# State-space stage of a two-layer decoder trunk: order of chunks, skip term, clears and products

## The reference, cut to what matters

```python
lam_bar = jnp.exp(lam * dt)
b_bar = ((lam_bar - 1.0) / lam)[..., None] * b
bu = jnp.einsum('gpn,bsgn->bsgp', b_bar, uf)
_, states = lax.associative_scan(combine, (a, bu), axis=1)   # x_t = lam_bar * x_(t-1) + bu_t
y = jnp.einsum('gnp,bsgp->bsgn', c, states).real + d_skip * uf
g = jax.nn.gelu(y)
out = g * jax.nn.sigmoid(g @ w_glu + b_glu)
```

## Time and profile before

| what | value |
|---|---|
| median of 3 runs | 1474.73 us (1473.92 to 1476.48) |
| the profiled execution | 1474.49 us, its span 1472.8 us |
| TensorE busy | 1439.1 us (98%) |
| VectorE busy | 1191.7 us (81%) |
| ScalarE busy | 978.0 us (66%) |
| GpSimd busy | 100.2 us (7%) |
| mean granted TensorE clock | 0.991 |
| DMA | 425.95 MB, mean 289 GB/s |

### The profile page before, as it was taken

One profiled execution on the slowest core, in us unless ns is written; L12 is line 12 of the kernel. 1 busy time (PEld: TensorE's weight loads), 2 busy tenths in 40 slices (PEclk: granted clock), 3 DMA queues, 4 the chain that ended last, 5 costly groups with the idle time before them and its releaser, 6 DMA issues.

```text
span 1472.8 us, 20745 instructions
## 1 busy us (share of the span) xinstructions
PE 1439.1 (98%) x7832; PEld 1209.2 (82%) x7832; DVE 1191.7 (81%) x1190; ACT 978.0 (66%) x954; POOL 100.2 (7%) x130
## 2 busy tenths in 40 slices
PE   8989999999989999999999999999999999999997
PEld 4678799998869888888888888888888888888886
DVE  6895455555777988988898898888889889888887
ACT  5326444444674777877777777787787777778775
POOL 1753100000240000000000000000000000000000
PEclk9999999999999999999999999999999999999999
DMA  8437655443326999999999999999999999999992
GB/s 230 145 71 260 236 192 185 147 155 115 121 109 233 349 370 371 331 362 375 337 351 360 348 357 366 378 323 363 373 337 358 366 343 349 370 373 331 359 376 94
DMA packets 193088, 425.95 MB, mean 289 GB/s; under 512 B 14002, under 2 KB 23088, under 8 KB 192944
## 3 DMA queue, kind: packets, MB, share of 16 engines
q1 hardware_dynamic: 192480, 424.35, 80.3%
q10 hardware_dynamic: 560, 0.94, 0.3%
HBM read 421.67 MB, written 1.05 MB: 287 GB/s over the span
## 4 chain that ended last, share of the span: by engine, by line
PE 91%; ACT 2%; POOL 1%; DVE 1%; issue 1%; ACTq 1%; DMA 1%; SPq 1%; DVEq 0%
PE bank L425 78%; PE bank L447 3%; PE bank L908 2%; PE bank L490 2%; PE bank L920 1%; PE bank L700 1%; PE bank L529 1%; PE bank L453 1%; ACTq L1021 1%; SPq L1081 1%; POOL work L1171 1%; ACT w_hi L1531 1%; DMA ring<-work 1%; PE bank L626 1%; DVE ring L1697 0%
## 5 line engine op out<-in xcount | busy, mean ns | idle before, releaser
L2015 DVE TENSOR_TENSOR w_lo<-ring,w_hi 128x2048 fp32r<-128x2048 f32 x341 | 777.7, 2290 | 99.6 <-ACT w_hi L1531 98.2
L1531 ACT ACTIVATE w_hi<-ring 128x2048 fp32r<-128x2048 f32 x341 | 649.1, 1917 | 129.1 <-PE bank L425 126.1
L425 PE MATMUL bank<-w_hi,xg_hl 128*128 128x512 f32 x1792 | 557.1, 392 | 0.0
L425 PEld LDWEIGHTS bank<-w_hi,xg_hl 128*128 128x128 f32 x1792 | 332.8, 188 | 67.2
L425 PE MATMUL bank<-w_lo,xg_hl 128*128 128x512 f32 x896 | 349.4, 390 | 0.0
L425 PE MATMUL bank<-w_hi,at_hl 128*128 128x512 f32 x896 | 277.5, 391 | 0.0
L425 PEld LDWEIGHTS bank<-w_lo,xg_hl 128*128 128x128 f32 x896 | 168.2, 188 | 35.8
L425 PEld LDWEIGHTS bank<-w_hi,at_hl 128*128 128x128 f32 x896 | 167.1, 188 | 33.9
L425 PE MATMUL bank<-w_lo,at_hl 128*128 128x512 f32 x448 | 174.5, 389 | 0.0
L1888 DVE TENSOR_TENSOR fpart_hl<-ring,fpart_hl 128x1024 fp32r<-128x1024 f32 x66 | 80.6, 1224 | 75.1 <-ACT fpart_hl L1439 74.9
L425 PE MATMUL bank<-ht_hl,fpart_hl 128*128 128x256 f32 x1056 | 128.0, 283 | 0.0
(11 more groups left out here) (253 smaller groups left out, 1151.7 us busy)
## 6 DMA issues: line engine op xcount, KB each, us to landing
ring<-in_l_moe_w_gate SPq DMA_DIRECT2D x58, 2048.0 KB, 8.0
ring<-in_l_moe_w_up SPq DMA_DIRECT2D x57, 2048.0 KB, 7.9
ring<-in_l_moe_w_down SPq DMA_DIRECT2D x56, 2048.0 KB, 7.9
ring<-in_l_ffn_w_gate SPq DMA_DIRECT2D x5, 2048.0 KB, 9.0
ring<-in_l_ffn_w_up SPq DMA_DIRECT2D x5, 2048.0 KB, 7.9
ring<-in_l_ffn_w_down SPq DMA_DIRECT2D x5, 2048.0 KB, 7.5
ring<-in_l_w_in SPq DMA_DIRECT2D x4, 2048.0 KB, 9.3
ring<-in_l_w_out SPq DMA_DIRECT2D x4, 2048.0 KB, 8.7
```

The lines of the kernel that those rows point to most:

```text
L425: last = mm(p, lhsT=xs[a], rhs=ws[b], start=start and q == 0, stop=stop and q == 2, **kw)
L1531: ac(w_hi(n), at(e_slot(q) * SLOT + j * HALF, HALF), ACT.Copy).then_inc(S("hi"), 1)
L2015: tt(LO[e_slot(q)][:, j * HALF:(j + 1) * HALF], at(e_slot(q) * SLOT + j * HALF, HALF), w_hi(n).bitcast(fp), ALU.subtract).then_inc(S("lo"), 1)
```

## The change

Chunk order: inside Ug, V, VX and Xbd the 32 chunks are ordered "(r b)", the step in a block outermost, so that the same step of all 8 blocks is contiguous. The Ug copies put them in that order as they read PSUM, and the gelu reads them back from it. Shifting by one chunk now takes two copies per half instead of one.

Skip term: 24 small products of an identity with MD (32 rows, 16 columns each) are added to K in PSUM; GpSimd's add is gone. K's products wait for the sums of CA by pairs instead of for all.

Tiles: Tm lies where Wt was, and Kst, Ysb and Xbd lie where Bm was, so that Tm can be cleared before V is computed. Clears: GpSimd clears half of Tm; ScalarE clears the other half in front of its V copies, and Xbd in two halves, in front of its K copies and in front of its Toeplitz DMAs.

Order: the queries' squares go behind the keys' ones, after the scan; the power steps go in front of the wait for V; on TensorE the carried products go in front of the Toeplitz ones, which now finish the banks; on GpSimd the first keys' root goes in front of the queries' one.

```diff
-        Tm = at(18432, 2, STEPS * PAIRS * GDIM)
+        Tm = at(B0, 2, STEPS * PAIRS * GDIM)
...
-        Kst = at(B0, STEPS, PAIRS, GDIM, rows=32)
+        Kst = at(18432, STEPS, PAIRS, GDIM, rows=32)
...
-        Ysb = at(B0, STEPS, PAIRS * GDIM, rows=64)
-        Xbd = at(B0 + 3072, 2, PAIRS, 64)
+        Ysb = at(18432, STEPS, PAIRS * GDIM, rows=64)
+        Xbd = at(18432 + 3072, 2, PAIRS, 64)
...
@@ tensor: K
-            pe.wait_ge(S("s5_ca"), 12)
+            pe.wait_ge(S("skip"), 1)
...
             for jq in range(6):
                 c0 = jq % 4 * P
+                pe.wait_ge(S("s5_ca"), 2 * jq + 2)
                 for ri in range(2):
                     for a in range(4):
                         mm(kb[jq // 4][32 * a:32 * a + 32, c0:c0 + GDIM], lhsT=W0bd[:, ri, jq * 4 + a], rhs=cT[:, ri, jq * 4 + a],
-                           start=(jq % 4 == 0 and ri == 0), stop=(ri == 1), skip_group_check=True)
+                           start=(jq % 4 == 0 and ri == 0), stop=False, skip_group_check=True)
+                for a in range(4):
+                    mm(kb[jq // 4][32 * a:32 * a + 32, c0:c0 + GDIM], lhsT=ident[0:32, 0:32], rhs=MD[:, jq * 4 + a],
+                       start=False, stop=True, skip_group_check=True)
...
@@ tensor: Y
+            yb = [unit(pe, ("Y", n), n) for n in range(3)]
+            pe.wait_ge(S("xbd"), 12)
+            for n in range(3):
...
+                            mm(yb[n][64 * jh:64 * jh + 64, a * P:(a + 1) * P], lhsT=Xbd[:, ri, j], rhs=CA[:, ri, j],
+                               start=(a == 0 and ri == 0), stop=False, skip_group_check=True)
             pe.wait_ge(S("tm"), 16 * 16)
...
-            pe.wait_ge(S("xbd"), 4)
...
@@ toeplitz
-            eng.wait_ge(S("kst_d"), 1)
-            eng.wait_ge(S("tm_zero"), 1)
+            for n in range(2):
+                read_out(eng, ("K", n))
+            eng.wait_ge(S("tm_zero"), 2)
...
@@ gpsimd
-            got(pool, ("V", 2))
-            g.memset(Tm, 0.0).then_inc(S("tm_zero"), 1)
-            g.memset(Xbd, 0.0).then_inc(S("xbd_zero"), 1)
-            for n in range(2):
-                read_out(pool, ("K", n))
-            g.tensor_tensor(Kst[:, 0], Kst[:, 0], MD, ALU.add).then_inc(S("kst_d"), 1)
+            got(pool, ("Bm", 11))
+            g.memset(Tm[:, 1], 0.0).then_inc(S("tm_zero"), 1)
+            root("mk0", 1, hss[:, 0:8], hrs[:, 0:8], HD)
             root("q0", 1, hss[:, 16:24], hrs[:, 16:24], HD)
-            root("mk0", 1, hss[:, 0:8], hrs[:, 0:8], HD)
...
@@ scalar
+            def clear(x, n):
+                return ac(x.rearrange("p (a b) -> p a b", b=P), ident.unsqueeze(1).to_broadcast([P, n // P, P]), ACT.Copy, scale=0.0)
...
-                    free(ac(Ug[:, n * 4:n * 4 + 16], p[:, :].rearrange("p (a c) -> p a c", a=16), ACT.Copy), ("Ug", n // 4))
+                    free(ac(Ug[:, n * 4:n * 4 + 16].rearrange("p a (r b) -> p a r b", r=SL),
+                            p[:, :].rearrange("p (a b r) -> p a r b", a=16, r=SL), ACT.Copy), ("Ug", n // 4))
...
+            act.wait_ge(S("s5_w0"), 4)
+            clear(Tm[:, 0], STEPS * PAIRS * GDIM).then_inc(S("tm_zero"), 1)
             for n in range(3):
                 p = got(act, ("V", n))
...
+            clear_carried(0)
             for n in range(2):
                 p = got(act, ("K", n))
...
+            clear_carried(1)
             toeplitz(act, 1)
             act.wait_ge(S("scan"), 1)
-            act.wait_ge(S("xbd_zero"), 1)
+            act.wait_ge(S("xbd_zero"), 2)
             for g2 in range(2):
-                ac(Xbd[g2 * 64:(g2 + 1) * 64, 1, :, g2 * 32 + 1:g2 * 32 + 32], VX[g2 * 64:(g2 + 1) * 64, 1, :, 0:31],
-                   ACT.Copy).then_inc(S("xbd"), 1)
+                g_ = slice(g2 * 64, (g2 + 1) * 64)
+                ac(Xbd[g_, 1, :, g2 * 32 + SB:g2 * 32 + CHUNKS], VX[g_, 1, :, 0:CHUNKS - SB], ACT.Copy).then_inc(S("xbd"), 1)
+                ac(Xbd[g_, 1, :, g2 * 32 + 1:g2 * 32 + SB], VX[g_, 1, :, CHUNKS - SB:CHUNKS - 1], ACT.Copy).then_inc(S("xbd"), 2)
...
-                    last = ac(GT6[:, g2 * 3 + n].rearrange("p (c k) -> p c k", k=STEPS),
-                              p[:, :].rearrange("p (k g c) -> p g c k", k=STEPS, g=2)[:, g2], ACT.Gelu_apprx_tanh)
+                    last = ac(GT6[:, g2 * 3 + n].rearrange("p (b r k) -> p b r k", r=SL, k=STEPS),
+                              p[:, :].rearrange("p (k g r b) -> p g b r k", k=STEPS, g=2, r=SL)[:, g2], ACT.Gelu_apprx_tanh)
...
@@ vector: steps_and_squares (the four lines go behind head_norm of "mk0", after the scan)
-                for h in range(2):
-                    for m in range(TM):
-                        read_out(dve, ("win0", h, m))
-                head_norm([(heads_of(HS[:, m, MAIN:D]), 4) for m in range(TM)], 8, "q0", 16, sq0, None)
...
-            for n in range(3):
-                read_out(dve, ("V", n))
             read_out(dve, "q_pw")
             next_powers(0, 1, 0)
             next_powers(0, 2, 1)
-            XB = VX.rearrange("p i j (b r) -> p (i j) b r", r=SL)
+            for n in range(3):
+                read_out(dve, ("V", n))
+            XB = VX.rearrange("p i j (r b) -> p (i j) r b", r=SL)
...
             for r in range(1, SL):
-                carry(0, 0, SB, XB[:, :, :, r - 1], XB[:, :, :, r])
+                carry(0, 0, SB, XB[:, :, r - 1], XB[:, :, r])
```

More of the change, by code:

```diff
@@ L660, in _ @@
             proj_kv("memkv1", MT[1], "mkv1", (6, 7))
+            yb = [unit(pe, ("Y", n), n) for n in range(3)]
+            pe.wait_ge(S("xbd"), 12)
+            for n in range(3):
+                for a in range(4):
+                    for ri in range(2):
+                        for jh in range(2):
+                            j = 8 * n + 4 * jh + a
+                            mm(yb[n][64 * jh:64 * jh + 64, a * P:(a + 1) * P], lhsT=Xbd[:, ri, j], rhs=CA[:, ri, j],
+                               start=(a == 0 and ri == 0), stop=False, skip_group_check=True)
             pe.wait_ge(S("tm"), 16 * 16)
-            yb = [unit(pe, ("Y", n), n) for n in range(3)]
             for n in range(3):
@@ L669, in _ @@
                             r0 = 64 * jh + 32 * g2
-                            mm(yb[n][r0:r0 + 32, a * P:(a + 1) * P], lhsT=Ug[:, g2 * PAIRS + j], rhs=Tj[:, g2, j],
-                               start=(a == 0), stop=False, skip_group_check=True)
-            pe.wait_ge(S("xbd"), 4)
-            for n in range(3):
[L674 to L679, removed]
+                            last = mm(yb[n][r0:r0 + 32, a * P:(a + 1) * P], lhsT=Ug[:, g2 * PAIRS + j], rhs=Tj[:, g2, j],
+                                      start=False, stop=True, skip_group_check=True)
                 ready(last, ("Y", n))
@@ L1327, in _, with clear_carried @@
                 free(ac(dst, src, ACT.Copy), ("V", n))
+            def clear_carried(ri):
+                clear(Xbd[:, ri].rearrange("p j c -> p (j c)"), PAIRS * 64).then_inc(S("xbd_zero"), 1)
+            clear_carried(0)
             for n in range(2):
@@ L1730, in steps_and_squares @@
                     v.tensor_copy(U5[:, :, s * GDIM:(s + 1) * GDIM], U4[:, s].rearrange("p (g i) -> p g i", i=GDIM)).then_inc(S("u5_dve"), 1)
-                for q in range(4):
-                    read_out(dve, ("memT", q))
-                for h in range(2):
-                    for m in range(TM):
-                        read_out(dve, ("win0", h, m))
-                head_norm([(heads_of(HS[:, m, MAIN:D]), 4) for m in range(TM)], 8, "q0", 16, sq0, None)
             for ri in range(2):
@@ L1784, in _ @@
             for r in range(1, SL):
-                carry(0, 0, SB, XB[:, :, :, r - 1], XB[:, :, :, r])
+                carry(0, 0, SB, XB[:, :, r - 1], XB[:, :, r])
             for b in range(1, SB - 1):
-                carry(SL - 1, b, 1, XB[:, :, b - 1:b, SL - 1], XB[:, :, b:b + 1, SL - 1])
+                carry(SL - 1, b, 1, XB[:, :, SL - 1, b - 1:b], XB[:, :, SL - 1, b:b + 1])
             for r in range(SL - 1):
-                carry(r, 1, SB - 1, XB[:, :, 0:SB - 1, SL - 1], XB[:, :, 1:SB, r])
+                carry(r, 1, SB - 1, XB[:, :, SL - 1, 0:SB - 1], XB[:, :, r, 1:SB])
             v.memset(stp[:, 0, 0, 0:1], 0.0).then_inc(S("scan"), 1)
@@ L1792, in _ @@
             for g2 in range(2):
-                v.tensor_copy(Xbd[g2 * 64:(g2 + 1) * 64, 0, :, g2 * 32 + 1:g2 * 32 + 32],
-                              VX[g2 * 64:(g2 + 1) * 64, 0, :, 0:31]).then_inc(S("xbd"), 1)
+                g_ = slice(g2 * 64, (g2 + 1) * 64)
+                v.tensor_copy(Xbd[g_, 0, :, g2 * 32 + SB:g2 * 32 + CHUNKS], VX[g_, 0, :, 0:CHUNKS - SB]).then_inc(S("xbd"), 1)
+                v.tensor_copy(Xbd[g_, 0, :, g2 * 32 + 1:g2 * 32 + SB], VX[g_, 0, :, CHUNKS - SB:CHUNKS - 1]).then_inc(S("xbd"), 2)
             dve.wait_ge(S("ld_hg"), 192)
@@ L1803, in _ @@
             head_norm([(heads_of(MKR[0].rearrange("p a b -> p (a b)")), 8)], 8, "mk0", 0, sqk, None)
+            for h in range(2):
+                for m in range(TM):
```

(3 more changed lines are left out.)

## The result

The changed kernel takes 1464.2 us (median of 5, 1462.86 to 1468.32) beside 1474.79 us in the same comparison: ratio 0.9932, 95% interval [0.9915, 0.9948]. So the gain is 6 to 10 us, and 7 to 8 is the better estimate (medians of all 18 executions of the changed kernel 1466.5 us, of the 78 of the kernel before in the later comparisons 1474.2); 3.3 were forecast. The profiled execution took 1466.02 us, its span is 1464.3.

The account below looks back on a forecast made before the run. TensorE, last to end, bounds the kernel for 91% of the span. Its products start at 104.1 instead of 107.44 us, 3.3 us gained with nothing added behind: 1471.4 us from 1474.73, range 1468.8 to 1474.6.

Parts of the forecast that it names:

- the products' own time: TensorE's Toeplitz and carried products: the clock falls again in 2.8 us of idling, so they stay at 9.7 us.
- ScalarE, instruction by instruction: ScalarE's copies and clears priced singly; query copies (1.07) and a clear (1.5) precede its Toeplitz issues, which start at 91.85.
- SP's head start: SP's Toeplitz issues start 2.5 us ahead, shortening ScalarE's 11.29 us queue stay by up to 2.5; middle: free at 102.0.
- rival B: TensorE idles less before the Y products and the clock doesn't fall: 6.0 us gained, 1468.7 us; chance 0.10.
- The skip term: 24 small products joining K on TensorE cost 0.6 us, at most 1.7; GpSimd's add (1.00) and its wait fall away.
- The start of the stage: Moving the queries' squares on VectorE: K gains 0.25 of 1.9 us, V stays, scan starts 1.8 us earlier, about 83.1.
- The scan: VectorE's scan, contiguous instead of at a step of four floats: 24.2 us become 18.1, saving 6.1, ending at 101.2.
- Rival D: The step isn't what slows VectorE's scan, but the repeated coefficient or port: scan stays 24.2 us, 1476.7 us; chance 0.08.
- The clears and copies: ScalarE's clears cost 2.8 us (Tm half) and 1.5 (Xbd half), Ug copies nothing more, its four Xbd copies 2.04.
- Behind Y: After the Y products nothing is added or lost; ScalarE's 1.28 us table load stays in the chain.

Follow-up runs that it names:

- e6: Changed kernel with ScalarE waiting for its own two Xbd clears in front of its Toeplitz DMA issues instead of behind them: 1469.1 us, ratio 0.9970.
- e8: Changed kernel with the queries' squares back in front of the CA products: ratio 0.9961 to the kernel before.
- e7: Changed kernel with the skip term added by GpSimd again and without the 24 small products: ratio 0.9958 to the kernel before.
- e3: Changed kernel with the chunks in natural order again (scan at a step of four floats, one shifting copy): ratio 1.0014 to the kernel before.
- e10: Same kernel as e7 (changed kernel, skip term on GpSimd again), run once more: ratio 0.9964 to the kernel before.
- e13: Kernel before, with 22 unread identity products in TensorE's wait in front of the Toeplitz products: 1472.0 us beside 1473.5, ratio 0.9992.
- e11: Changed kernel with the skip term on GpSimd again and 26 unread identity products in TensorE's wait: ratio 0.9958 to the kernel before.
- e1: The kernel before, unchanged, run and traced once more: ratio 1.0001.
- e2: The changed kernel, unchanged, run and traced once more: ratio 0.9950 to the kernel before.
- e9: The changed kernel, unchanged, as the measure for other runs of its call: ratio 0.9940 to the kernel before.
- e5: Kernel before plus the chunk layout alone, with its copies and the gelu's reading: ratio 1.0000.

## Why the prediction was wrong

The direction and the mechanism held: both chains had to move, the scan's and the DMAs', and Y starts behind ScalarE's copies. Two steps failed. The larger in us is the products' own time: the forecast put the clock's share at nothing, and it measured 1.5 to 2.8 us. The other is ScalarE's issues, put behind copies that they don't wait for. Together with V's place in the first trace it made Y's start 1.5 us too late. These are the terms:

- **ScalarE, instruction by instruction: a failed step.** The forecast let ScalarE "first copy the queries (1.07) and clear (1.5)" before its DMA issues, at 91.85. Nothing makes them wait: an issue goes out when its own semaphores are met, beside copies that were started or queued ahead of it. The issue stood 0.08 us behind the last K copy. Put right with the forecast's own numbers, the queue is free at 89.2 + 0.1 + 11.3 = 100.6, the scan's 101.2 counts, and Y starts at 103.3: +38.5 instead of +39.3, so 0.8 us of the 1.5 by which +39.3 missed +37.8. The other 0.7 is the start of the scan, below. e6, with the wait written in, shows the price of a real one (2.4 us).
- **SP's head start.** It fell away with the same step: both queues start together, and ScalarE's is held for 11.3 us as before, ending with the scan to 0.1 us. Where the head start exists (e6) it is worth 0.5 us and not the 1.2 that is in the middle of 102.0.
- **The products' own time: the larger failed step.** The forecast kept 9.7 us, since it saw 2.8 us of idling in the new kernel. The wait was 0.3 us, and all four traces of the changed kernel took 8.2. Of the kernel before the traces have 9.7 and 11.0. So what came is rival B, which had a chance of 0.10: the clock stayed up, 1.5 to 2.8 us, after a shorter wait than even B assumed (2.0). That the shorter wait is the reason is supported and not shown: the clock fell in the waits of 2.9 (e8), 3.5 (e7) and 5.4 us (e3), and not in those of 0.3 to 2.2 us (e6 the longest), but not in e10's 3.8 either. Its start of 103.3 is also what the step above gives when put right. That the products' gain is passed on to the end is supported by e13's median and not shown by its interval.
- **The skip term.** Forecast 0.6 us, at most 1.7; measured 2.6 to 2.8 (e7, e10): each of the six groups is 0.30 us longer, and 0.7 to 1.1 us is a gap among the L582 products of the last group for which no trace names a releaser. It stands in all four traces of the changed kernel, and at this place in none of those without the small products (e7, e10, e11); its cause is open. The mis-sizing did no harm, since TensorE waited there anyway. It is also why TensorE's wait shrank to 0.3 us: without it (e7, e10) the wait is 3.5 to 3.8 us and the clock falls in one trace of two.
- **The start of the stage.** V was forecast not to move, and it stands at +10.5 in the traces of both kernels (e1, e2), and at +11.7 only in the first one, which had the stretch at half clock. By this the forecast, worked out from the first trace, had the scan's start at +18.3 (83.1) where it was at +17.6: the 0.7 us named above. The move of the squares, priced at 0.25 us for K and 1.8 for the scan, was worth 2.3 us at the start of the scan and the same at Y, and nothing for K (e8). K starts 1.6 to 2.2 us earlier (+16.3 for +17.9 to +18.5), with the squares back as without; what is left for that is its waiting for the sums by pairs, which no run undoes.
- **The scan.** Forecast 18.1 us, measured 18.1. Of the 6.1 us the layout gave 5.4 (e3 takes 23.5); the other 0.7 is one add that took 1.62 us instead of 0.90 beside GpSimd's skip-term add (at 90.4 us in the first trace). GpSimd's add is gone from the changed kernel; with it back (e7), the scan is 0.7 us longer again. Rival D fell with e3 and with the rows. The power steps took 0.8 us more than before, beside GpSimd's last sums, and the scan started 0.6 us behind the last V copy (80.35 to 80.94).
- **The clears and copies.** 2.76 and 1.48 us for 2.8 and 1.5; Ug's copies kept 0.60 us at the new step; the four Xbd copies took 1.86 for 2.04. The Toeplitz products didn't wait.
- **Behind Y** nothing was added up to the gated unit, and the table load is on the chain, as forecast; it is worth 0.3 to 0.7 us and not 1.28, as the next thing is TensorE's transposes. The profiled execution alone lost 1.6 us to half clock in the gated unit, the like of what e13's rival foretold; the three later traces of the changed kernel did not.

The trace agrees with one half of the note that the prediction weighed (the Trainium skill, SBUF — State Buffer, section "Door 1: The DMA port swizzle"): a step of four floats never hits a 16-byte line twice, and costs 1.9 ns an element instead of 1.04. It disagrees with the other half, that four fp32 elements may be stridden for free.

In sum, on the traces: 4.9 us of earlier start (+42.7 to +37.8) and 1.5 to 2.8 us of clock, 6.4 to 7.7 us, beside 6.4 to 7.4 us between the medians of the three later comparisons. The granted clocks of the single executions say the same in another way, and account for the surplus of the first comparison (10.6 us) as far as it can be seen. At a mean clock of 0.994 both kernels occur: 14 executions of the kernel before with a mean of 1472.0 us, 6 of the changed one with 1467.5, so 4.5 us at equal clock, near the 4.9 of Y's start. Over all, the kernel before has 0.987 to 0.994 and a mean of 1474.1 us, the changed one 0.993 to 0.997 and 1466.1. So some 3.5 of the 8.0 us go with a higher clock; this is an estimate, as the clocks have three places. They are not all won in the Y products: a stretch at half clock near 160 us stands in all four traces of the kernel before and its variants, and near 150 in only two (e2, e9) of the four of the changed one. In the first comparison three of five executions had 0.997 (1462.9 to 1464.2 us), in the later ones three of 13 (1464.3 to 1464.6). Why one execution gets 0.997 and another 0.994 stays open.

## What to carry to other kernels

Where two chains end within a few microseconds of each other, price the change against both: here each half alone was worth nothing, in the order of products that it had, and the pair about 0.5%. A DMA issue of ScalarE waited here for its semaphores and for the issues ahead of it, and not for the copies that precede it in the engine's program (0.08 us behind the last K copy, and 2.5 with a semaphore in between); look at whether a semaphore stands between before pricing them in. And an engine's wait has two prices, its length and the clock that the engine has afterwards.

## What the runs showed of the hardware

- VectorE, fp32 in SBUF: with the 0.16 us that the forecast worked out as fixed taken off, a step of 16 bytes costs 1.8 to 1.9 ns an element on a product (1576 ns for 768 in e3, 1636 in the trace of before) and on an add (891 ns for 384 in e3), contiguous ones 1.04 (958 ns for 768). ScalarE reading PSUM at the same step pays nothing (0.60 us for 512 elements, as before).
- A VectorE product or add of two SBUF tiles beside GpSimd's add of 1.0 us took 0.7 to 0.8 us longer: 1.62 us for 0.90 (before), 1.15 for 0.34 (e5), 1.24 for 0.56 (e7). Beside GpSimd's clear of Tm the scan's instructions kept their times (0.56 and 0.90 us in the trace of before).
- 24 products of 32 rows and 16 columns, packed between other small ones, cost 2.6 to 2.8 us of TensorE (e7, e10); the cheapest row for such a product would have made it 0.5. Of this 1.8 is in the groups (0.81 us from group to group instead of 0.51), the rest in a gap without a releaser.
- A ScalarE DMA issue started 0.08 us behind the K copy whose semaphore it needed, with a copy and a clear of its program still to run; eight such issues, beside eight on SP, held the queue for 11.3 us, and for 10.8 with SP 2.4 us ahead (e6).
- TensorE waited 3.5 us in one execution and the clock fell to 1.2 GHz, and 3.8 us in another of the same kernel and it stayed at 2.4 GHz (e7, e10). It also fell in a wait of 2.9 us (e8) and stayed in one of 2.2 (e6). A forecast that needs one of them has to carry both.
- The start of the kernel's state-space stage moved by 2.1 us between executions of one kernel (62.67 to 64.77), so stages are compared from a point inside the trace.
